# Forgetting, sliding-window and latent attention: one PSUM bank for a pair of heads, two banks by turns, one set of output operations for the pair

## The reference, cut to what matters

```python
pr = softmax(scores)                                # 128 queries x the keys they see
outs.append(jnp.einsum('bhqk,bhkd->bhqd', pr, vh))  # values: 64 columns per head
...
return (o * jax.nn.silu(z)) @ w_out                 # sliding and latent: gated, then projected
```

## Time and profile before

| what | value |
|---|---|
| median of three runs | 3825.61 us |
| profiled execution: time, span | 3830.3 us, 3828.2 us |
| TensorE busy | 3414.2 us, 89% of the span |
| VectorE busy | 2218.3 us, 58% |
| ScalarE busy | 1102.5 us, 29% |
| GpSimd busy | 1420.3 us, 37% |
| mean granted TensorE clock | 0.946 of full speed |
| 16 DMA engines | 77 GB/s over the span |

### The profile page before, as it was taken

The page is one execution under the profiler, slowest core; times in us unless marked ns, Lnnn a source line. Parts: engine busy times, 40 slices in busy tenths (PEclk is TensorE's granted clock), DMA queues, the critical chain, the costliest instruction groups (busy, mean ns, idle before and its releaser), DMA issues.

```text
span 3828.2 us, 45399 instructions
## 1 busy us (share of the span) xinstructions
PE 3414.2 (89%) x16179; PEld 2672.8 (70%) x16179; DVE 2218.3 (58%) x3073; ACT 1102.5 (29%) x1795; POOL 1420.3 (37%) x694
## 2 busy tenths in 40 slices
PE   6999998899999999998899999877788778887898
PEld 5888766678887788776578887665555456655676
DVE  5443497774434544368775443589764567565663
ACT  1222233422223322233332222321234422332322
POOL 3444453344444444454334444321132113211342
PEclk9999999899999999999899999987799889988899
DMA  3333331223332333332133333332321112211221
GB/s 98 96 89 95 95 80 41 66 88 94 92 91 89 96 94 89 102 89 61 31 88 93 97 88 99 71 107 64 107 65 55 34 39 72 53 35 39 79 83 55
DMA packets 623130, 296.39 MB, mean 77 GB/s; under 512 B 96941, under 2 KB 618798, under 8 KB 622990
## 3 DMA queue, kind: packets, MB, share of 16 engines
q1 hardware_dynamic: 620734, 289.69, 27.3%
q0 software_dynamic: 1360, 2.63, 0.2%
q10 hardware_dynamic: 896, 2.23, 0.2%
HBM read 287.65 MB, written 6.84 MB: 77 GB/s over the span
## 4 chain that ended last, share of the span: by engine, by line
PE 72%; DVE 22%; issue 3%; ACT 2%; POOL 1%; DMA 1%; DVEq 0%; SPq 0%; ACTq 0%; POOLq 0%
PE ps L328 22%; PE ps L319 22%; PE ps L320 21%; DVE Y L1596 4%; PE ps L1017 2%; PE ps L1006 1%; PE ps L982 1%; DVE NM L1031 1%; DVE SS L421 1%; DVE T L2500 1%; PE ps L489 1%; DVE UL L743 0%; DVE UL L412 0%; DVE TURN L418 0%; DVE T L752 0%
## 5 line engine op out<-in xcount | busy, mean ns | idle before, releaser
L257 POOL TENSOR_TENSOR WL<-RAW,WH 128x1024 fp32r<-128x1024 f32 (+4 forms) x606 | 1313.0, 2168 | 2281.4 <-ACT WH L279 2281.3
L319 PE MATMUL ps<-UH,WH 128*128 128x512 f32 x3056 | 1242.6, 407 | 101.4 <-DVE UL L743 35.9
L320 PE MATMUL ps<-UL,WH 128*128 128x512 f32 x3056 | 1217.0, 398 | 0.0
L279 ACT ACTIVATE WH<-RAW 128x1024 fp32r<-128x1024 f32 (+4 forms) x605 | 571.2, 945 | 1375.9 <-PE ps L328 1347.0
L328 PE MATMUL ps<-UH,WL 128*128 128x512 f32 x3056 | 780.6, 398 | 11.1 <-POOL WL L257 11.1
L319 PEld LDWEIGHTS ps<-UH,WH 128*128 128x128 f32 x3056 | 589.9, 193 | 272.4 <-issue 49.5
L328 PEld LDWEIGHTS ps<-UH,WL 128*128 128x128 f32 x3056 | 579.1, 191 | 143.9 <-POOL WL L257 13.6
L320 PEld LDWEIGHTS ps<-UL,WH 128*128 128x128 f32 x3056 | 589.4, 193 | 128.8 <-issue 5.4
L1502 DVE TENSOR_TENSOR T<-ps,R 128x512 f32<-128x512 f32 x88 | 60.8, 691 | 392.7 <-PE ps L328 392.7
L319 PE MATMUL ps<-HH,WH 128*128 128x512 f32 x704 | 279.2, 397 | 0.0
L320 PE MATMUL ps<-HL,WH 128*128 128x512 f32 x704 | 276.9, 393 | 0.0
(11 more groups left out here) (432 smaller groups left out, 3599.4 us busy)
## 6 DMA issues: line engine op xcount, KB each, us to landing
RAW<-w_ff_in SPq DMA_DIRECT2D x176, 512.0 KB, 3.8
RAW<-w_in SPq DMA_DIRECT2D x72, 512.0 KB, 3.9
RAW<-w_ff_out SPq DMA_DIRECT2D x64, 384.0 KB, 3.4
RAW<-w_ff_out SPq DMA_DIRECT2D x64, 320.0 KB, 3.2
RAW<-d_w_in SPq DMA_DIRECT2D x24, 512.0 KB, 3.7
RAW<-b_w_in SPq DMA_DIRECT2D x17, 512.0 KB, 3.8
RAW<-w_out SPq DMA_DIRECT2D x16, 512.0 KB, 4.1
RAW<-w_ple_gate SPq DMA_DIRECT2D x16, 512.0 KB, 4.1
```

The lines of the kernel that those rows point to most:

```text
L257: e.tensor_tensor(m.WL[:, s, 0:k, :], m.RAW[:, r, 0:k, :], m.WH[:, s, 0:k, :].bitcast(F32), ALU.subtract).then_inc(m.low_ready.sem, 1)
L279: e.activation(m.WH[:, s, 0:k, :], m.RAW[:, r, 0:k, :], ACT.Copy).then_inc(m.high_ready.sem, 1)
L319: e.matmul(out, m.WH[:, s, c, 0:t.cols], H[:, k0 + c, :], start=(x == 0 and c == 0), stop=False)
L320: e.matmul(out, m.WH[:, s, c, 0:t.cols], L[:, k0 + c, :], start=False, stop=False)
```

## The change

Both heads of a pair put their values into the same bank, the even head into partitions 0 to 63, the odd one into 64 to 127. Pairs use banks 6 and 7 by turns. TensorE waits, before the first value matmul of a pair, for the pair before the last. `heads_out` waits for both heads and empties them with one operation of 128 partitions (forgetting) or three (sliding, latent). `head_out` counts pairs.

```diff
-        self.h0 = m.head_out.reserve(heads)
+        self.h0 = m.head_out.reserve(heads // 2)
...
-                if n == 0 and self.h0 + h > 0:
-                    e.wait_ge(m.head_out.sem, self.h0 + h)
+                if n == 0 and self.h0 + h // 2 > 1:
+                    e.wait_ge(m.head_out.sem, self.h0 + h // 2 - 1)
                 nb = self.blocks(n)
                 for j in range(nb):
                     for p in range(2):
-                        mm = e.matmul(m.ps[HD * p:HD * p + HD, 6 + p, n * P:(n + 1) * P], self.v(h + p, n, j),
+                        mm = e.matmul(m.ps[HD * p:HD * p + HD, 6 + h // 2 % 2, n * P:(n + 1) * P], self.v(h + p, n, j),
                                       self.buf.PT[:, p, j * P:(j + 1) * P], start=(j == 0), stop=(j == nb - 1))
...
-        for a in (2 * s, 2 * s + 1):
-            h, p0 = self.block(a)[0], HD * (a % 2)
-            e.wait_ge(m.valued.sem, self.b + a + 1)
-            self.freed = (m.head_out.sem, self.h0 + h + 1)
-            self.out(self, e, h, m.ps[p0:p0 + HD, 6 + h % 2, :], p0)
+        c = s // TT
+        e.wait_ge(m.valued.sem, self.b + 2 * s + 2)
+        self.freed = (m.head_out.sem, self.h0 + c + 1)
+        self.out(self, e, c, m.ps[:, 6 + c % 2, :])
...
-            def out_head(g, e, h, ps, p0):
-                e.tensor_copy(QKV[p0:p0 + HD, 2 * CC + h // 2, :], ps).then_inc(*g.frees())
+            def out_heads(g, e, c, ps):
+                e.tensor_copy(QKV[:, 2 * CC + c, :], ps).then_inc(*g.frees())
...
-        def gated_head(z, head0=0):
-
-            def f(g, e, h, ps, p0):
-                c = (head0 + h) // 2
-                r = slice(p0, p0 + HD)
+        def gated_heads(z, high, low):
+
+            def f(g, e, c, ps):
                 e.wait_ge(*v.last)
-                e.tensor_tensor(m.T[r, :], ps, z[r, c, :], ALU.mult).then_inc(*v.next())
+                e.tensor_tensor(m.T[:], ps, z[:, c, :], ALU.mult).then_inc(*v.next())
                 e.wait_ge(*v.last)
-                e.tensor_copy(m.UH[r, c, :], m.T[r, :]).then_inc(*v.next())
+                e.tensor_copy(high[:, c, :], m.T[:]).then_inc(*v.next())
                 e.wait_ge(*v.last)
-                e.tensor_tensor(m.UL[r, c, :], m.T[r, :], m.UH[r, c, :].bitcast(F32), ALU.subtract).then_inc(*g.frees())
+                e.tensor_tensor(low[:, c, :], m.T[:], high[:, c, :].bitcast(F32), ALU.subtract).then_inc(*g.frees())
```

More of the change, by code:

```diff
@@ L1723, in mixer @@
             half_of = lambda h: slice(HD * (h % 2), HD * (h % 2) + HD)
-            def out_head(g, e, h, ps, p0):
-                e.tensor_copy(QKV[p0:p0 + HD, 2 * CC + h // 2, :], ps).then_inc(*g.frees())
+            def out_heads(g, e, c, ps):
+                e.tensor_copy(QKV[:, 2 * CC + c, :], ps).then_inc(*g.frees())
             att = Heads(m, B, HEADS, q=lambda h, n: head(0, h, slice(n * P, (n + 1) * P)),
                         k=lambda h, n: head(CC, h, slice(0, (n + 1) * P)),
-                        v=lambda h, n, j: V[:, j, h * HD:(h + 1) * HD], out=out_head,
+                        v=lambda h, n, j: V[:, j, h * HD:(h + 1) * HD], out=out_heads,
                         add=lambda h, n: (PICK[half_of(h), h:h + 1].to_broadcast([HD, P]), CUM2[half_of(h), 0:(n + 1) * P]), mask=MASKB[:],
@@ L1825, in mixer @@
                           [(co, {"tensor": 16, "scalar": 10, "vector": 8})], rhs_ready=s_att)
-            first.needs = [(m.head_out.sem, att.h0 + HEADS)]
+            first.needs = [(m.head_out.sem, att.h0 + HEADS // 2)]
             add(first)
@@ L2598, in silu @@
                 return e.activation(ZB[:, c, :], ZB[:, c, :], ACT.Silu)
[L2600 to L2607, removed]
             first = lambda n: max(n - 1, 0) * P
@@ L2613, in swa @@
                             v=lambda h, n, j: VB[:, max(n - 1, 0) + j, HD * (h // 8):HD * (h // 8) + HD],
-                            out=gated, scale=HD ** -0.5, bias=lambda h, n: BIAS[:, h, P * (2 - nb(n)):2 * P],
+                            out=gated_heads(ZB, ZH, QL), scale=HD ** -0.5, bias=lambda h, n: BIAS[:, h, P * (2 - nb(n)):2 * P],
                             sink=lambda h: SINK[:, h:h + 1], gate=silu, blocks=nb, needs=[(m.flip_free.sem, m.flips.total)])
@@ L2712, in mla @@
             att = LatentHeads(m, B3, MLA_HEADS, q=lambda h, n: QM[0:QK, h % 8, n * P:(n + 1) * P], k=lambda h, n: KM[0:QK, h % 8, 0:(n + 1) * P],
-                              v=lambda h, n, j: VM[:, j, h % 8 * HD:(h % 8 + 1) * HD], out=gated_head(ZC), mask=MASKB[:],
+                              v=lambda h, n, j: VM[:, j, h % 8 * HD:(h % 8 + 1) * HD], out=gated_heads(ZC, m.UH, m.UL), mask=MASKB[:],
                               turn=lambda h, t: VT(h // 2 % 4)[:, t * P:(t + 1) * P], to=lambda h, ts: VM[:, ts, h % 8 * HD:(h % 8 + 2) * HD],
```

## The result

| | before | after |
|---|---|---|
| median of the runs shown, us | 3826.25 (4 runs, 3824.17 to 3832.28) | 3680.75 (4 runs, 3677.58 to 3681.88) |
| ratio to before | | 0.9616 (95%: 0.9599 to 0.9633) |
| profiled execution: its time, its span, us | 3830.3, 3828.2 | 3681.88, 3680.1 |
| mean granted clock | 0.946 | 0.963 |

The change takes off 145.5 us; the forecast was 141 us and 3685 us.

The account below looks back on a forecast made before the run. The bound was TensorE's 20 waits between pairs, 114.4 us, and the slow-clock stretches behind them. Terms 43 + 40 + 38.4 + 14 + 5.3 = 141 us off 3825.6 gave 3685 us, range 3668 to 3711.

Parts of the forecast that it names:

- Latent, five turns: Latent attention, five turns with a GEMM tile behind: 8.6 us each from wait, tile and value matmuls, 43 us.
- Sliding window, five turns: Sliding-window attention, five turns with a GEMM tile behind: wait and slow stretch, about 8 us each, 40 us.
- Forgetting: Forgetting attention, three turns per layer: 5.7, 8 and 5.5 us, 19.2 per layer, 38.4 us for two layers.
- Last two turns and the end: Sliding and latent stages: two turns each without a GEMM tile, 3.5 us per turn, plus 1.95 us at each stage's end.
- Everything outside the stages unchanged: A sign of being right: nothing outside the attention stages changes, 0 us there.
- Part 2: Half the emptying operations: 37 us of VectorE work goes, almost all beside TensorE; 5.3 us on the path at stage ends.
- part 1: Two banks by turns: a pair's first value matmul waits for the pair before the last, a wait without length.
- Part 3: Value matmuls of both heads into two halves of one bank: taken as 0 us, bounds 0 and 188 us.
- alternating halves: Rival: side-by-side running is lost in one bank, 54 ns more per value matmul instruction, 47 us, 3731 us; chance 0.05.
- slower kernel: Rival: the second half's value matmul waits until the first half's ends, 188 us lost against 141 won, 3873 us; chance 0.03.
- New waits take the place: Rival: exponentials or normalisations become late once TensorE no longer rests, 3742 to 3789 us; chance 0.09.
- The clock falls all the same: Rival: remaining short waits bring TensorE's clock down, so the clock term, 16 turns, some 31 us, fails: 3716 us; chance 0.07.

Follow-up runs that it names:

- cross_banks: Against the changed kernel: each head emptied by its own 64-partition operations, the odd head in the other of the two banks; 3705.67 us, ratio 0.9683.
- one_bank_busy16: Against the changed kernel: all pairs in bank 6, waiting for the pair before, 16 extra matmuls into bank 7 ahead of each turn's wait; 3739.98 us.

## Why the prediction was right, step by step

- **What bounds it.** Right. The 20 waits of the earlier trace rows and the slow stretches behind them were the gain: all 20 are gone, and line 1017 waits for no operation of VectorE.
- **Latent, five turns: 43 us.** The one turn followed, 31.4 us to 22.7, gave 8.7 us against 8.6. The later four gave 8.4 to 8.1, so the five together 41.4 us: the first is the best of them.
- **Sliding window, five turns: 40 us.** The five turns of the ledger, each from just before its wait to just before the next, give 8.4, 6.3, 8.4, 8.6 and 6.6, together 38.4 us.
- **Forgetting: 38.4 us, and 1.4 for the two ends.** Measured 40.3, 38.0 and 41.5 us in the three traces. The prediction costed the turns by what would be late next, not by their waits. The sum held, the single turns less so: for 5.7, 8.0 and 5.5 + 0.7 us the ledger of layer 0 gives 4.5, 6.7 and 6.6.
- **Last two turns and the end.** 9 us were predicted for each stage. In the sliding stage the ledger leaves 45.9 less 38.4, 7.5 us (7.2 and 7.9 in the two other traces). In the latent stage it leaves 53.1 less 41.4, 11.7 us, and 13.1 and 13.2 in the others: 3 to 4 us more than predicted.
- **Everything outside the stages unchanged.** Wrong, by 6.8 us at two places, where VectorE and GpSimd meet. No step of the prediction looked for what else a shift in time would trigger. The 6.8 us are luck, a shift that fell the right way. The sum stays close without them: the forecast of 3685 us was 4 us too high, and would have been 3 us too low.
- **Part 2: "Almost all of it (37 us) lies beside TensorE once part 1 is there".** This step failed, and only an experiment showed it: with the operations doubled again, at two banks by turns, 30 us are lost. By the ledger about 9 of them lie between the forgetting layers, the luck of the row above; most of the others lie in the sliding stage (7.4 us), the latent stage (5 to 7) and layer 1 (3 to 5): the maxima of the next scores stand behind the emptying, and TensorE is back for them sooner than the prediction allowed. The sum hid the error, since part 1 had been costed with the saved operations already in place: the turn was followed with VectorE free at 3331.1, after three operations and not after six.
- **Part 3: one bank costs nothing.** Shown by cross_banks, within what the runs can tell; with it fall the rivals of alternating halves and of the slower kernel.
- **New waits take the place.** They hardly grow: the largest left in the sliding stage are 11.0 us in ten at line 1006, for ScalarE. In the forgetting stage of layer 0, with VectorE at 90%, TensorE's waits for `S` at line 982 go from 5.5 to 6.9 us.
- **The clock falls all the same.** Refuted: 0.97 in all three stages as long as GEMM tiles run. The rule of the Trainium skill that the prediction weighed (TensorE: Matmul & The Clock Gate, "A second HAM failure mode: psum-queue depth-cycling") did not show here: going through two banks by turns took idle spells away, and raised the mean clock from 0.946 to 0.963. The clock term itself was sized too low: 31 us for 16 turns, 1.9 each, where one_bank_busy16 measured 43 us for 20, 2.2 each, though with waits of 4 us and not 6.
- **The granted clock above 0.95 in three stages.** Right for two. For the sliding stage as a whole it is 0.88, because of the last 43 us at 0.68. The price of that was already in the small sum for the last two turns.
- **The range.** 3668 to 3711 us held, but its source does not give it: 1.5 us more or less on each of twenty turns are 30 us either way, 3655 to 3715.

## What to carry to other kernels

Where an engine waits for a buffer to be emptied, a second buffer is worth more than a faster emptying: 116 us against 42 here, and together less than their sum. Follow one period in the timeline and ask what is late next, and cost every part on its own too, or errors of two parts hide in their sum. Count an idle spell of TensorE twice, the spell and the slow stretch behind it, here 2.2 us behind waits of about 4 us. To tell the two apart, fill the wait with matmuls into an unused bank, and never with more than the wait holds.

## What the runs showed of the hardware that had not been expected

- An addition of VectorE on 128x512 took 2.85 us instead of 0.68 us when it began 0.06 us after a GpSimd operation of 128x1024; begun 0.12 us before it, VectorE took its 0.68 us and GpSimd 2.80 instead of 2.37 us. In these rows the one that starts first keeps its time or nearly so, and the other ends after it. The Trainium skill (GPSIMD Engine Reference, "1. Specifications") says that GpSimd shares its SBUF interfaces with VectorE, with contention for VectorE's instructions with two SBUF inputs; these rows agree.
- TensorE busy with useless work through a wait made a kernel 43 us faster (3783.27 to 3739.98 us). Nearly twice that work made it 10 us slower (3793.22 us).
